# A hybrid encoder layer: the router's turnings and logits between the halves of a tile's products, pair 2 chosen within tile 7

## What is computed

```python
x = x + concat(NA, RWKV, MEM) @ W_out
h = rms_norm(x, ffn_norm_w)
glogits = h @ w_group + b_group            # 4 groups: the largest one
elogits = h @ w_expert + b_expert          # 4 experts in the group: the two largest
weights = softmax(glogits)[group] * top_2(softmax(elogits[group])) / their sum
x = x + sum over the two chosen experts of weights * (silu(h @ w_gate) * (h @ w_up)) @ w_down
```

## Time and profile before

| | us |
|---|---|
| median of 3 runs | 1319.21 (1316.09 to 1319.23) |
| the profiled execution, its own time | 1308.68 |
| its span, first to last instruction | 1307.0 |
| TensorE (PE) busy | 1188.6 (91%) |
| VectorE (DVE) busy | 549.0 (42%) |
| ScalarE (ACT) busy | 297.8 (23%) |
| GpSimd (POOL) busy | 201.5 (15%) |

### The profile page before, as it was taken

The page is one execution under the profiler, slowest core; times in us unless marked ns, Lnnn a source line. Parts: engine busy times, 40 slices in busy tenths (PEclk is TensorE's granted clock), DMA queues, the critical chain, the costliest instruction groups (busy, mean ns, idle before and its releaser), DMA issues. The chain is left out here.

```text
span 1307.0 us, 23913 instructions
## 1 busy us (share of the span) xinstructions
PE 1188.6 (91%) x9764; PEld 672.5 (51%) x9764; DVE 549.0 (42%) x1300; ACT 297.8 (23%) x760; POOL 201.5 (15%) x248
## 2 busy tenths in 40 slices
PE   6999999999998898988989999299999999998783
PEld 5544444444444666988954556144444444444342
DVE  4368255889793556555743344211211111111010
ACT  5162216222203677323421222000000000000000
POOL 0201310300001333000000011301012333321121
PEclk9999999999998899999999998599999999999887
DMA  8411521322103633356206415248989898989990
GB/s 310 106 28 46 174 65 53 104 89 97 49 32 110 159 100 89 92 173 201 59 2 228 193 65 191 70 159 308 376 332 382 328 384 333 382 321 384 398 347 26
DMA packets 108419, 239.99 MB, mean 184 GB/s; under 512 B 36116, under 2 KB 71396, under 8 KB 102936
## 3 DMA queue, kind: packets, MB, share of 16 engines
q1 hardware_dynamic: 91704, 190.15, 40.8%
q0 software_dynamic: 16608, 48.33, 10.9%
HBM read 208.89 MB, written 36.10 MB: 187 GB/s over the span
## 5 line engine op out<-in xcount | busy, mean ns | idle before, releaser
L492 PE MATMUL pj_ps<-hT,pj_w 128*128 128x512 f32 x576 | 253.1, 595 | 0.0
L492 PEld LDWEIGHTS pj_ps<-hT,pj_w 128*128 128x128 f32 x576 | 108.3, 190 | 134.0 <-issue 133.5
L1921 PE MATMUL ex_py<-wd,ex_hT 128*128 128x512 f32 x256 | 112.6, 593 | 1.0 <-DVE proj L2047 1.0
L1380 PE MATMUL ps_out<-w_out,mixT 128*128 128x512 f32 x256 | 111.9, 594 | 0.3 <-PEq L1387 0.3
L2078 DVE TENSOR_TENSOR ex_hid<-ex_pu,ex_sg 128x512 f32<-128x512 f32 x16 | 11.1, 692 | 206.8 <-PE ex_pu L1941 206.8
L2005 ACT ACTIVATE ex_sg<-ex_pg 128x512 f32<-128x512 f32 x16 | 9.6, 597 | 319.2 <-PE ex_pg L1933 319.2
L699 DVE RECIPROCAL mixT<-mixT 128x1024 f32<-128x1024 f32 (+1 forms) x11 | 68.9, 6262 | 25.7 <-ACT mixT L620 25.7
L1380 PEld LDWEIGHTS ps_out<-w_out,mixT 128*128 128x128 f32 x256 | 48.1, 190 | 58.5 <-issue 58.4
L1921 PEld LDWEIGHTS ex_py<-wd,ex_hT 128*128 128x128 f32 x256 | 47.6, 190 | 55.2 <-issue 54.0
L1535 POOL DMA_INDIRECT slot_tokens<-op_entry,op_slot x16 | 15.6, 972 | 304.5 <-DVE op_slot L1646 300.8
L1933 PE MATMUL ex_pg<-proj 128*128 128x512 f32 x128 | 59.1, 617 | 1.3 <-DVE proj L2040 1.3
(11 more groups left out here) (303 smaller groups left out, 1970.1 us busy)
## 6 DMA issues: line engine op xcount, KB each, us to landing
wd<-in_moe_w_down SPq DMA_DIRECT2D x21, 2048.0 KB, 9.6
proj<-in_moe_w_gate SPq DMA_DIRECT2D x11, 2048.0 KB, 14.8
proj<-in_moe_w_up SPq DMA_DIRECT2D x11, 2048.0 KB, 20.4
mixT<-in_moe_w_gate SPq DMA_DIRECT2D x10, 2048.0 KB, 14.8
mixT<-in_moe_w_up SPq DMA_DIRECT2D x10, 2048.0 KB, 20.4
pj_w<-in_w_in SPq DMA_DIRECT2D x18, 512.0 KB, 4.0
products<-pj_unit POOLq DMA_DIRECT2D x4, 2048.0 KB, 10.3
proj<-products SPq DMA_DIRECT2D x32, 256.0 KB, 3.4
```

Of the source, the lines that this page charges most:

```text
L492: mm = pe.matmul(ps[:, t % 2, half, :], w_tile(t)[:, n, :], s.hT[:, n, half * 512:(half + 1) * 512], start=(n == 0), stop=(n == KD - 1))
L1380: mm = pe.matmul(s.ps_out[:, t % 2, half * 512:(half + 1) * 512], s.mixT[:, k, t * P:(t + 1) * P], s.w_out[:, k, half * 512:(half + 1) * 5 ...
L1921: mm = pe.matmul(py[:, half, :], hT[:, j, :], wd[e % 2][:, j, half * 512:(half + 1) * 512], start=(j == 0), stop=(j == KF - 1))
```

## The change

TensorE's stream no longer has one step per tile. After tile 1 the turning of tile 0 stands between the halves of tile 2, that of tile 1 after them. From tile 3 on, each tile is: logits of tile t - 2 (of tile 0 ahead of tile 3, of tile 1 within it), first half, in tiles 4, 5 and 7 (`CHOOSE`) the ranks of pairs 0, 1 and 2, turning of tile t - 1, second half. VectorE and ScalarE follow the same order: VectorE adds the bias ahead of a tile's additions, chooses and weighs ahead of the first addition and places between the two; ScalarE makes the exponentials ahead of the copy and the root of that tile. Pair 0 was chosen after tile 3 and ranked after tile 4's products; pair 1 was chosen after tile 5 and ranked after tile 6's. What each operation computes, the buffers, and the streams of SP and POOL are as before. The new file's lines from 1377 on lie up to 36 further down (L1668 is L1682 there, L1677 L1693, L1682 L1698, L1563 L1557, L1571 L1565, L1380 L1381).

The diff, with the bodies of two functions that only moved cut out:

```diff
--- before.py
+++ after.py
@@ -1372,6 +1372,7 @@
 
 ATTENTION, RWKV = (0, 1, 2, 3, 6, 7), (4, 5)
 EARLY = 2
+CHOOSE = (4, 5, 7)
 
 
 def out_products(pe, s, t, half, chunks):
@@ -1546,32 +1547,48 @@
                 pe.matmul(pl[:, 1, 0:2 * NE], s.before, flat, start=True, stop=True)
                 pe.matmul(pl[:, 1, 2 * NE:4 * NE], s.ones, flat, start=True, stop=True).then_inc(ranked, 1)
 
-            for t in range(TT + 2):
-                if t < TT:
-                    if t >= 2:
-                        pe.wait_ge(added, 2 * (t - 1))
-                    for half in range(2):
-                        out_products(pe, s, t, half, RWKV if t < EARLY else ATTENTION + RWKV).then_inc(done, 1)
-                if t >= 2:
-                    q = t - 2
-                    if q == 0:
-                        pe.wait_ge(router_in, 80)
-                    pe.wait_ge(copied, q + 1)
-                    if q:
-                        pe.wait_ge(biased, q)
-                    for k in range(KD):
-                        mm = pe.matmul(pl[:, 0, 0:NG + NE], hT[:, q % 2, k, :], wr[:, k, :], start=(k == 0), stop=(k == KD - 1))
-                    mm.then_inc(logits, 1)
-                if 1 <= t <= TT:
-                    q = t - 1
-                    pe.wait_ge(normed, q + 1)
-                    if q:
-                        pe.wait_ge(copied, q)
-                    for k in range(KD):
-                        mm = pe.transpose(pt[:, k, :], h[:, q % 2, k * P:(k + 1) * P], s.ident)
-                    mm.then_inc(turned, 1)
-                if t in (4, 6, 8):
-                    ranks(t // 2 - 2)
+            def logits_of(q):
+                if q == 0:
+                    pe.wait_ge(router_in, 80)
+                pe.wait_ge(copied, q + 1)
+                if q:
+                    pe.wait_ge(biased, q)
+                for k in range(KD):
+                    mm = pe.matmul(pl[:, 0, 0:NG + NE], hT[:, q % 2, k, :], wr[:, k, :], start=(k == 0), stop=(k == KD - 1))
+                mm.then_inc(logits, 1)
+
+            def turn(q):
+                pe.wait_ge(normed, q + 1)
+                if q:
+                    pe.wait_ge(copied, q)
+                for k in range(KD):
+                    mm = pe.transpose(pt[:, k, :], h[:, q % 2, k * P:(k + 1) * P], s.ident)
+                mm.then_inc(turned, 1)
+
+            def products(t, half):
+                out_products(pe, s, t, half, RWKV if t < EARLY else ATTENTION + RWKV).then_inc(done, 1)
+
+            for t in range(2):
+                for half in range(2):
+                    products(t, half)
+            pe.wait_ge(added, 2)
+            products(2, 0)
+            turn(0)
+            products(2, 1)
+            turn(1)
+            for t in range(3, TT):
+                logits_of(0 if t == 3 else t - 2)
+                pe.wait_ge(added, 2 * (t - 1))
+                products(t, 0)
+                if t == 3:
+                    logits_of(1)
+                if t in CHOOSE:
+                    ranks(CHOOSE.index(t))
+                turn(t - 1)
+                products(t, 1)
+            logits_of(TT - 2)
+            turn(TT - 1)
+            logits_of(TT - 1)
             ranks(PAIRS - 1)
 
         @block.vector
@@ -1658,35 +1675,46 @@
             link(dve.tensor_copy(entry[:, :, :, ROW_READ], token))
             dve.tensor_copy(entry[:, :, :, ROW_WRITE], token).then_inc(tok_ready, 1)
             link(dve.memset(s.count[:, :], 0.0))
-            for t in range(TT + 2):
-                if t < TT:
-                    if t % 2 == 0:
-                        dve.wait_ge(s.x1_in[t // 2], 16)
-                    for half in range(2):
-                        dve.wait_ge(done, 2 * t + half + 1)
-                        x = s.x1[:, t, half * 512:(half + 1) * 512]
-                        dve.tensor_tensor(x, s.ps_out[:, t % 2, half * 512:(half + 1) * 512], x, ALU.add).then_inc(added, 1)
-                    dve.wait_ge(rooted, t + 1)
-                    dve.reciprocal(st[:, t % 2, 2:3], st[:, t % 2, 1:2]).then_inc(inverted, 1)
-                    dve.wait_ge(inverted, t + 1)
-                    if t == 0:
-                        dve.wait_ge(router_in, 80)
-                    if t >= 2:
-                        dve.wait_ge(turned, t - 1)
-                        dve.wait_ge(rows_out[t % 2], 16 * (t // 2))
-                    dve.scalar_tensor_tensor(out=by_run(h[:, t % 2, :], KD), in0=interleaved(s.x1[:, t, :], KD), scalar=st[:, t % 2, 2:3],
-                                             in1=interleaved(wf[:, :], KD), op0=ALU.mult, op1=ALU.mult).then_inc(normed, 1)
+            def add(t, half):
+                dve.wait_ge(s.x1_in[t // 2], 16)
+                dve.wait_ge(done, 2 * t + half + 1)
+                x = s.x1[:, t, half * 512:(half + 1) * 512]
+                dve.tensor_tensor(x, s.ps_out[:, t % 2, half * 512:(half + 1) * 512], x, ALU.add).then_inc(added, 1)
+
+            def norm(t):
...
+            def bias(q):
+                dve.wait_ge(logits, q + 1)
+                dve.tensor_tensor(lg[:, q, :], pl[:, 0, 0:NG + NE], br[:, :], ALU.add).then_inc(biased, 1)
+
+            for t in range(TT):
+                if t >= 3:
+                    bias(0 if t == 3 else t - 2)
+                if t in CHOOSE:
+                    dve.wait_ge(biased, 2 * CHOOSE.index(t) + 2)
+                    choose(CHOOSE.index(t))
+                    weigh(CHOOSE.index(t))
+                add(t, 0)
+                if t == 3:
+                    bias(1)
+                if t in CHOOSE:
+                    place(CHOOSE.index(t))
+                add(t, 1)
+                norm(t)
+            for q in (TT - 2, TT - 1):
+                bias(q)
+            dve.wait_ge(biased, TT)
+            choose(PAIRS - 1)
             weigh(PAIRS - 1)
             place(PAIRS - 1)
 
@@ -1699,25 +1727,33 @@
                 act.wait_ge(second_peak, g + 1)
                 act.activation(e2v[:, :], e2v[:, :], ACT.Exp).then_inc(second_exp, 1)
 
-            for t in range(TT + 2):
-                if t < TT:
-                    act.wait_ge(added, 2 * t + 2)
-                    if t >= 2:
-                        act.wait_ge(inverted, t - 1)
-                    if t:
-                        act.wait_ge(summed, t)
-                    act.activation(sq[:, :], s.x1[:, t, :], ACT.Square, accum_out=st[:, t % 2, 0:1]).then_inc(summed, 1)
-                    act.wait_ge(summed, t + 1)
-                    act.activation(st[:, t % 2, 1:2], st[:, t % 2, 0:1], ACT.Sqrt, bias=s.eps, scale=1.0 / D).then_inc(rooted, 1)
-                if 1 <= t <= TT:
-                    q = t - 1
-                    act.wait_ge(turned, q + 1)
-                    if q >= 2:
-                        act.wait_ge(logits, q - 1)
-                    act.activation(hT[:, q % 2, :, :].rearrange("p a b -> p (a b)"), pt[:, :, :].rearrange("p a b -> p (a b)"),
-                                   ACT.Copy).then_inc(copied, 1)
-                if t in (3, 5, 7, 9):
-                    exponents((t - 3) // 2)
+            def copy(q):
+                act.wait_ge(turned, q + 1)
+                if q >= 2:
+                    act.wait_ge(logits, q - 1)
+                act.activation(hT[:, q % 2, :, :].rearrange("p a b -> p (a b)"), pt[:, :, :].rearrange("p a b -> p (a b)"),
+                               ACT.Copy).then_inc(copied, 1)
+
+            def root(t):
...
+            for t in range(TT):
+                if t in CHOOSE:
+                    exponents(CHOOSE.index(t))
+                if t >= 2:
+                    copy(0 if t == 2 else t - 1)
+                root(t)
+                if t == 2:
+                    copy(1)
+            copy(TT - 1)
+            exponents(PAIRS - 1)
 
 
 def expert_loads(s, e, u):
```

More of the change, by code:

```diff
@@ L1660, in _ @@
             link(dve.memset(s.count[:, :], 0.0))
-            for t in range(TT + 2):
-                if t < TT:
-                    if t % 2 == 0:
-                        dve.wait_ge(s.x1_in[t // 2], 16)
-                    for half in range(2):
-                        dve.wait_ge(done, 2 * t + half + 1)
-                        x = s.x1[:, t, half * 512:(half + 1) * 512]
-                        dve.tensor_tensor(x, s.ps_out[:, t % 2, half * 512:(half + 1) * 512], x, ALU.add).then_inc(added, 1)
-                    dve.wait_ge(rooted, t + 1)
-                    dve.reciprocal(st[:, t % 2, 2:3], st[:, t % 2, 1:2]).then_inc(inverted, 1)
-                    dve.wait_ge(inverted, t + 1)
-                    if t == 0:
-                        dve.wait_ge(router_in, 80)
-                    if t >= 2:
-                        dve.wait_ge(turned, t - 1)
-                        dve.wait_ge(rows_out[t % 2], 16 * (t // 2))
-                    dve.scalar_tensor_tensor(out=by_run(h[:, t % 2, :], KD), in0=interleaved(s.x1[:, t, :], KD), scalar=st[:, t % 2, 2:3],
```

(40 more changed lines are left out.)

1 line of the change is left out of this document (removed).

## The result

Eight timed runs of each kernel: the change takes a median of **1326.09 us** (1318.60 to 1329.57), the kernel before 1315.47 us (1314.03 to 1319.23). The ratio is **1.0071, with a 95% interval of 1.0048 to 1.0095**, so the change costs 9.3 us (6.3 to 12.5). The ratio is not that of the two medians, which lie 10.6 apart. The forecast was +8.8. The profiled execution of the change took 1324.37 us (span 1322.7).

The account below looks back on a forecast made before the run. TensorE's chain bounds the kernel, through the router's last bias. Waits and tail +5.4 and clock +3.4 gave +8.8 us on 1319.21, so 1328.0; range from just above Rival B's lower end to Rival C's +12.1, rounded up.

Parts of the forecast that it names:

- What bounds the kernel: TensorE is busy 91% of the span; the change's whole effect is the shift of the router's last bias, 816.95.
- Products of tile 2 sooner: Tile 0's turning no longer stands ahead of tile 2's products, so they begin 2.6 us sooner.
- The wait in tile 3: TensorE waits 3.0 us ahead of tile 1's logits for tile 0's bias, held by tile 0's late row store.
- The waits for the choice: Ranks in tiles 4, 5 and 7 wait for VectorE's `both`: 0.75, 2.05 and 0.75, sum 3.55 us.
- The tail: From the last products to the last bias: 12.8 us in place of 15.1, so -2.3.
- All waits and the tail: Products end 7.7 us later and the tail is 2.3 shorter: +5.4 us before any clock loss.
- The clock: Falls to half near 730.8 in tile 3's gap: logits +0.9, turning +0.9, following products 1.6, in all +3.4 us.
- the bounds of 0 and 4.8: Lowest and highest price in us allowed for the clock's fall in tile 3, around the +3.4 taken.
- Rival B: Tile 0's row lands by 724.8, so tile 3's wait goes: +2.4 us, or -0.3 with the tail at full clock; chance 0.14.
- Rival C: The clock falls in tile 5's 3.3 us gap too: another 1.6 to 3.3 us, up to +12.1; chance 0.11.
- Adding to the median: The +8.8 us was added to 1319.21, the median of three timed runs of the kernel before, giving 1328.0.

Follow-up runs that it names:

- Run 6: Rows of tiles 0 and 1 stored ahead of the expert weights: in the change stage 149.95 us, ratio 1.0023; in the kernel before 145.45, 0.9994.
- Run 2: The change with the ranks of pairs 0 to 2 behind their tile's second half, and placing with them; stage 150.26 us, ratio 1.0025 to the kernel before.
- run 3: The change with the root's table loaded right after each choice, by an unused extra root; stage 151.52 us, ratio 1.0042 to the kernel before.
- run 5: The change with unread products in two gaps, three in tile 3 and two ahead of tile 5's ranks; stage 150.88 us, ratio 1.0046 to the kernel before.
- run 4: The change with three unread 512-column products in tile 3's wait, ahead of tile 1's logits; stage 152.70 us, ratio 1.0051 to the kernel before.
- run 1: The change with tile 3 whole again, then tile 2's turning and tile 1's logits; stage 149.76 us, ratio 1.0055 to the kernel before.
- run 7: The change with tile 3 whole, ranks behind second halves and early table load: stage 146.04 us, ratio 1.0000; with unread products in the tail 144.43, 0.997.

## Why the prediction was right

It said +8.8, slower; the runs say +9.3 (6.3 to 12.5), and once more +10.7 (7.2 to 14.1). The direction and the terms +5.4 are right by mechanism. That the total came within 0.5 is in part luck: the clock's term is twice what the two profiles of the change show, and their stage is 7.0 longer, not 8.8. By its steps:

- **What bounds the kernel.** Held. The stage's +7.03 is the last bias's +7.13; what lies between moved by 0.1.
- **Products of tile 2 sooner.** Forecast 2.6, measured 2.58.
- **The wait in tile 3.** Forecast 3.0, measured 2.58, with the releaser that was named: the bias behind the normalisation behind the store. The row landed 31.3 us into the stage in place of 31.8, which is the difference. Run 6 took away the store's delay and the wait went.
- **The waits for the choice.** Forecast 0.75, 2.05, 0.75 = 3.55; measured 0.70, 2.13, 0.82 = 3.65. Run 2 took away their cause, run 3 the table load's share in the middle one.
- **The tail.** Forecast 12.8, measured 12.84.
- **All waits and the tail.** Forecast +5.4, measured +5.64 in run 5, where the clock held.
- **The clock.** That it would fall in tile 3 was right. "I take 1.6, ... +3.4" is the term that was mis-sized: the profiled executions of the change show **1.7**, twice. The fall came at 737.5, when 1.5 us of logits had already passed, so these lost 0.37 and not 0.9; and the products lost 0.54, not 1.6, since it was back after 3.4 us. The step that was wrong is to put the products' 1.6 on top of the 1.8 of logits and turning. The 1.6 was read at 1205, and there too the clock was down for 3.4 us only, as windows of the kernel before show:

```profile
1205.00:1205.50 0.50, 0.26 (x2) 0.29 (x4) 0.00 (x0) 0.00 (x0) 0.00 (x0) 0.53 1.01 426
...
1208.00:1208.50 0.50, 0.50 (x6) 0.34 (x4) 0.00 (x0) 0.00 (x0) 0.00 (x0) 0.55 1.06 451
```

But there it fell 0.2 us ahead of the products, so nearly all of the 3.4 fell on them. In tile 3 it fell ahead of the rest of the logits and the turning, which took 2.3 of the 3.4, and 1.1 were left for the products. A sum of 3.4 us needs the clock down for 6.8. The same code in runs 2 and 3 had that and lost 3.4. The kernel before has falls of both lengths (3.4 us at 1205.0, 6.8 at 1222.1), so its profile didn't say which would come; the bounds of 0 and 4.8 held both.

- **Rival B** (the row lands earlier) did not come by itself. Made by hand in run 6, it gave 149.95, 4.7 over before, where the rival had said 2.4. Of the other 2.3, 1.7 is the clock in tile 5, which the rival did not count, and 0.4 that the wait taken away was 2.58 and not 3.0.
- **Rival C** did not come in the change. It came in runs 4 and 6, once tile 3 was cured. I had only put it on top of tile 3's loss.
- **Adding to the median.** The sum was put on 1319.21, but eight runs gave 1315.47 for the kernel before. The time 1328.0 was thus 1.9 above the 1326.09 measured, while the change of 8.8 was 0.5 below the 9.3 of the ratio and 1.8 below the 10.6 between the medians: the base that was too high made up for a change that was too small.

**What stays open.** The profiled executions account for 7.0 us in the stage, the timed runs say 9.3 and 10.7. The intervals hardly force a gap: 7.0 lies within the first (6.3 to 12.5) and just below the second (7.2 to 14.1), and the medians of the second lie 7.4 apart. If there is one, the clock may be it: runs 2 and 3 lost 3.4 in tile 3 where the profiled executions of the change lost 1.7. The profiled executions of the change are also among the shorter of its timed runs (1324.37 against a median of 1326.09, 1311.27 against 1314.53), and in the first eight the mean granted clock is 0.965 in the profiled one and 0.959 to 0.964 in the others. Run 5, whose profile has its clock up, is 6.0 over the kernel before by time (3.3 to 8.6) and 5.6 by its stage. But no clock by stage exists for the timed runs, so it isn't shown. What decides between a fall of 3.4 us and one of 6.8 stays open too. Why the store's row took 23 us was not split between the queue and the traffic: run 6 moved both at once.

## What to carry to other kernels

Moving a step earlier on an in-order engine is only as good as what the other engines have queued ahead of its inputs: follow each input back to its last releaser, here through a bias, a normalisation and a store behind 8 MB of weights, before the step is placed. Then count how long TensorE goes without wide products, whether it waits or does small matmuls, and look for the clock there and at the next such gap, since curing one may only move the loss. If an order loses by its waits, remove the causes and try it again: here the new order lost 0.7% with four waits, and with their causes gone (and the ranks put back) it won 0.24% (0.07 to 0.41).

## What was not expected of the hardware

- **Small matmuls did not hold the clock.** A turning and the logits of two tiles back to back, with TensorE busy by its records for all but 0.36 of 4.9 us, lost it in all three kernels that had them (runs 1 and both of run 7). The gap in tile 3, 5.2 us at full clock and half of it a wait, lost it in the change (twice) and in runs 2 and 3. The gap in tile 5, 3.5 us (2.13 of waiting, 0.47 of ranks, 0.91 of turning; the forecast had 3.3), lost it in runs 4 and 6 and kept it in the change (twice) and in run 1. The gaps of 2.7 us or less between the stage's products kept it in every profile. The Trainium skill, "TensorE: Matmul & The Clock Gate", Part 1, calls the slow level the default that activity releases; the falls beside a wait agree with that. The falls in the stretch that was almost all busy don't follow from it.
- **Among the stage's products it was down for about 3.4 or 6.8 us at a time**, in the same place of the same code (3.4 twice in the change, 6.8 in runs 2 and 3), and each time cost close to half of that: 1.7 or 3.4.
- **Unread products held it** wherever they were put: tile 3, tile 5 and the tail, where they made the last turning and logits 2.5 us shorter.
- **The start of a stage moves by 22 us between profiled executions** (689.2 to 711.2) with the code ahead of it unchanged. Two spans say little of a change of 9 us; the length of the stage, from the start of tile 1's products, was 152.27 and 152.40 in the two profiles of the change. Even it can differ by 1.7 with the clock, as tile 3 of runs 2 and 3 shows.
